# Sample scores as four groups of 24 rows, and both samples of a pair in one pass

## What is computed

```python
gate = einsum('hqd,hnd->hqn', qh, k_mean)              # mean key of each block of 256 keys
_, top = top_k(gate, n_top)                            # the 3 best of 4 past blocks
...
s = einsum('hqd,hqskd->hqsk', qh, kg) * scale
s = s - slopes[:, None, None, None] * (qpos - key_pos) # distance penalty
s = where(valid, s, -inf)
pr = softmax(s.reshape(ATT_HEADS, qc, -1), axis=-1).reshape(s.shape)
return einsum('hqsk,hqskd->hqd', pr, vg)
```

## Time and profile before

| what | value |
|---|---|
| time, median of 3 runs | 1353.81 us (1352.45 to 1355.06) |
| the profiled execution | 1353.38 us |
| its span from first to last instruction | 1351.7 us |
| TensorE busy with matmuls | 1322.9 us, 98% |
| VectorE, ScalarE, GpSimd busy | 57%, 49%, 17% |
| HBM traffic over the span | 173 GB/s |
| mean granted TensorE clock | 0.996 |

### The profile page before, as it was taken

One profiled execution on the slowest core, in us unless ns is written; L12 is line 12 of the kernel. 1 busy time (PEld: TensorE's weight loads), 2 busy tenths in 40 slices (PEclk: granted clock), 3 DMA queues, 4 the chain that ended last, 5 costly groups with the idle time before them and its releaser, 6 DMA issues.

```text
span 1351.7 us, 28355 instructions
## 1 busy us (share of the span) xinstructions
PE 1322.9 (98%) x11129; PEld 1276.1 (94%) x11129; DVE 772.7 (57%) x842; ACT 657.3 (49%) x741; POOL 233.4 (17%) x342
## 2 busy tenths in 40 slices
PE   6999999999999999999999999999999999999998
PEld 5999999999878999999999999999997799999998
DVE  5555555666556655554555555565755565555444
ACT  5555543434444655553355555333443555555434
POOL 4000000356440100000101000013755120000001
PEclk9999999999999999999999999999999999999998
DMA  6655544769787444444446654447797854444443
GB/s 198 206 175 163 167 141 157 191 184 228 184 279 224 143 155 155 142 134 157 158 130 193 186 177 134 156 147 208 182 243 223 255 173 156 140 150 155 141 144 128
DMA packets 213487, 235.27 MB, mean 174 GB/s; under 512 B 15006, under 2 KB 207272, under 8 KB 213396
## 3 DMA queue, kind: packets, MB, share of 16 engines
q1 hardware_dynamic: 205436, 211.19, 51.2%
q0 software_dynamic: 7840, 22.85, 6.0%
q10 hardware_dynamic: 120, 0.03, 0.0%
HBM read 228.83 MB, written 5.32 MB: 173 GB/s over the span
## 4 chain that ended last, share of the span: by engine, by line
PE 92%; issue 5%; DMA 1%; DVE 1%; POOLq 1%; SPq 0%; POOL 0%; ACT 0%; DVEq 0%; ACTq 0%
PE ps L1303 22%; PE ps L1304 22%; PE ps L1305 22%; PE ps L1390 4%; PE ps L1392 4%; PE ps L1391 4%; PE ps L1536 3%; PE ps L1573 2%; PE ps L1710 1%; PE ps L1712 1%; PE ps L1711 1%; PE ps L1431 1%; PE ps L1488 1%; DMA x_tok<-in_x_sample 0%; PE ps L1524 0%
## 5 line engine op out<-in xcount | busy, mean ns | idle before, releaser
L649 ACT ACTIVATE w_hi<-w_raw 128x2048 fp32r<-128x2048 f32 x170 | 325.4, 1914 | 538.6 <-PE ps L1305 421.0
L922 DVE TENSOR_TENSOR w_lo<-w_raw,w_hi 128x2048 fp32r<-128x2048 f32 x162 | 371.9, 2295 | 187.5 <-ACT w_hi L649 185.3
L1303 PE MATMUL ps<-h_hi,w_hi 128*128 128x320 f32 x768 | 239.4, 312 | 4.0 <-DVE x L989 2.3
L1305 PE MATMUL ps<-h_hi,w_lo 128*128 128x320 f32 x768 | 238.3, 310 | 0.0
L1304 PE MATMUL ps<-h_lo,w_hi 128*128 128x320 f32 x768 | 238.2, 310 | 0.0
L1303 PE MATMUL ps<-g_hi,w_hi 128*128 128x320 f32 x704 | 218.0, 310 | 0.0
L1305 PE MATMUL ps<-g_hi,w_lo 128*128 128x320 f32 x704 | 217.5, 309 | 0.0
L1304 PE MATMUL ps<-g_lo,w_hi 128*128 128x320 f32 x704 | 217.5, 309 | 0.0
L1303 PE MATMUL ps<-act_hi,w_hi 128*128 128x320 f32 x704 | 217.4, 309 | 0.0
L1304 PE MATMUL ps<-act_lo,w_hi 128*128 128x320 f32 x704 | 217.4, 309 | 0.0
L1305 PE MATMUL ps<-act_hi,w_lo 128*128 128x320 f32 x704 | 217.4, 309 | 0.0
(11 more groups left out here) (286 smaller groups left out, 1770.7 us busy)
## 6 DMA issues: line engine op xcount, KB each, us to landing
w_raw<-in_ffn_w_in SPq DMA_DIRECT2D x90, 1024.0 KB, 5.1
w_raw<-in_ffn_w_out SPq DMA_DIRECT2D x32, 896.0 KB, 4.6
w_raw<-in_w_in SPq DMA_DIRECT2D x22, 1024.0 KB, 6.0
kbuf<-in_cache_k SPq DMA_DIRECT2D x96, 192.0 KB, 4.9
w_raw<-in_ffn_w_out SPq DMA_DIRECT2D x16, 1024.0 KB, 5.0
kbuf<-in_cache_v SPq DMA_DIRECT2D x64, 192.0 KB, 3.9
w_raw<-in_w_out SPq DMA_DIRECT2D x8, 1024.0 KB, 6.6
kbuf<-in_cache_k POOLq DMA_DIRECT2D x32, 192.0 KB, 3.5
```

The costliest lines, as they stand in the source:

```text
L649: act.activation(w_hi[:, slot, :], w_raw[:, slot, :], ACT.Copy).then_inc(hi_done, 1)
L922: dve.tensor_tensor(w_lo[:, slot, :], w_raw[:, slot, :], w_hi[:, slot, :].bitcast(F32), ALU.subtract).then_inc(split_done, 1)
L1303: pe.matmul(out, w_hi[:, slot, w], hi[:, k, :], start=(k == 0), stop=False)
L1305: ins = pe.matmul(out, w_lo[:, slot, w], hi[:, k, :], start=False, stop=(k == k_all - 1))
```

## The change

- The rows of a pair are laid out as four groups of 32 partitions (sample bb, half of the heads), each with three heads of 8 queries and 8 unused rows: `alibi_s`, `alibi_own`, `rank`, `ss`, `sp` and `o_tok` grow from 96 to 128 partitions. `q_rep`, `q_bd` and `q_sc` get layouts to match; in `qprep`, `q_bd` takes 12 copies of 8 columns in place of 4 of 24.
- `key_scores(p)` and `smp_out(p)` do both samples in one go, on four column groups; the values go by 192 columns (three heads). `own_scores` has 8 matmuls in place of 6.
- `transpose_probs` transposes against all 128 columns of the identity, read with a step, so that the columns of the four groups are interleaved; `smp_out` reads its stationary operand with a step of 4. `transpose_out` becomes six matmuls of 16 columns.
- `sc_done`, `pv_done` and `o_evac` are raised once a pair. `next_k` waits for whole pairs, and SyncE issues `next_k(2, 1)` ahead of `mix_load(9)`.
- Value homes: samples 5 and 6 go to a new home E (`v_e`) and to D, both loaded by GpSimd; the load of sample 5 stands between `spread_v(3)` and `spread_v(4)`. SyncE loads sample 7 alone after pair 1. Both slots of `w_out` are loaded after pair 0.
- TensorE's order: `smp_out(3)` stands behind the first `out_part`, and the `early` parts of slot 1 are placed otherwise.

The constants, tile shapes and index helpers are left out of the diff below.

```diff
...
 
-        q_bd = sb("q_bd", [P, 3, 2, 32])
-        q_rep = sb("q_rep", [P, 4, 3, SMP])
+        q_bd = sb("q_bd", [P, 200])
...
+        v_e = at("v_e", [P, PAGES, HDIM], F32, arena_at, 12)
...
-        v_landed = {n: sem("v_landed_" + n) for n in "CWXABD"}
-        V_HOME = "XWBACDBA"
+        v_landed = {n: sem("v_landed_" + n) for n in "CWXABDE"}
+        V_HOME = "XWBACEDB"
...
-
-            return (6 if p else 4) + bb
+        def out_bank(p):
+
+            return (4, 6, 7, 6)[p]
 
         def page_numbers(engine, first, n):
 
...
 
-                    wait_apart(sp_e, sc_done, L * NB + (1 if p == 1 else p * 2 + (bb - 1)))
+                    wait_apart(sp_e, sc_done, L * (NB // 2) + p)
                     for half in range(2):
                         load_k(p, bb, half)
...
                 mix_load(8)
                 next_k(2, 0)
+                next_k(2, 1)
                 mix_load(9)
-                next_k(2, 1)
                 sp_e.wait_ge(u_out, 2 * L + 2)
                 sp_e.dma_start(O["pool_prompt"][bass.ds(L, 1), 0].rearrange("a t c -> (a t) c"),
...
                             sp_e.dma_start(v_page(u, 4 * half + j, slice(0, HDIM)),
                                            A["cache_v"][L, page[j]].rearrange("t h d -> t (h d)")).then_inc(v_landed[V_HOME[u]], 16)
 
+                wait_apart(sp_e, sc_done, (NB // 2) * L + 4)
                 for u in range(2, 4):
-                    wait_apart(sp_e, sc_done, NB * L + u + 5)
                     load_v(u)
+                wait_apart(sp_e, pv_done, (NB // 2) * L + 1)
                 for slot, cols in enumerate((slice(0, 256), slice(256, 512))):
-                    wait_apart(sp_e, pv_done, NB * L + 1 + slot)
                     square(A["w_out"], L, half0 + C_WO // 2, cols, slot, apart=True)
-                wait_apart(sp_e, pv_done, NB * L + 3)
-                load_v(6)
-                wait_apart(sp_e, pv_done, NB * L + 4)
+                wait_apart(sp_e, pv_done, (NB // 2) * L + 2)
                 load_v(7)
                 sp_e.wait_ge(st_prm, L + 1)
...
                     for bb in range(2):
-                        c = 16 * bb + 8 * half
-                        pool.tensor_copy(q_bd[HD * half:HD * half + HD, :, bb, c:c + 8],
-                                         q_smp[HD * half:HD * half + HD, :, p * 16 + 8 * bb:p * 16 + 8 * bb + 8])
+                        own = q_bd[HD * half:HD * half + HD, 96 * bb + 8 * half:96 * bb + 8 * half + 88]
+                        for f in range(3):
+                            pool.tensor_copy(own[:, 40 * f:40 * f + 8],
+                                             q_smp[HD * half:HD * half + HD, f, p * 16 + 8 * bb:p * 16 + 8 * bb + 8])
                 pool.drain()
-                for half in range(2):
-                    for bb in range(2):
-                        c = 16 * bb + 8 * half
-                        ins = pool.tensor_copy(q_sc[p][:, bb, :, half, :, c:c + 8],
-                                               q_rep[:, 2 * half:2 * half + 2, :, p * 16 + 8 * bb:p * 16 + 8 * bb + 8]
-                                               .rearrange("p j f q -> p f j q"))
+                for bb in range(2):
+                    for gg in range(2):
+                        at_g = 384 * bb + 192 * gg
+                        dst = q_sc[p][:, at_g:at_g + 216].rearrange("p (s x) -> p s x", s=3)[:, :, 0:64]
+                        ins = pool.tensor_copy(dst.rearrange("p s (j c) -> p s j c", j=2)[:, :, :, 0:8],
+                                               q_rep[:, 3 * gg:3 * gg + 3, :, p * 16 + 8 * bb:p * 16 + 8 * bb + 8])
                 ins.then_inc(qp_ok, 1)
 
...
                 spread_v(1)
                 wait_apart(pool, att_low, L + 1)
                 load_v_all(4)
-                for h in range(2, H):
-                    spread_v(h)
+                spread_v(2)
+                spread_v(3)
+                wait_apart(pool, r_done, H * L + H)
+                load_v_all(5)
+                spread_v(4)
+                spread_v(5)
                 wait_apart(pool, vbd_used, H * L + H)
                 wait_apart(pool, pt2_done, NB * L + 4)
-                load_v_all(5)
+                load_v_all(6)
                 add_squares(L * 12 + 8)
                 add_squares(L * 12 + 12)
...
 
-                def out_evac(p, bb):
+                def out_evac(p):
                     act.wait_ge(rs_ok, L * 4 + p + 1)
-                    act.wait_ge(pv_done, L * NB + p * 2 + (bb + 1))
-                    act.activation(o_tok[p % 2][:, bb, :], ps[0:96, out_bank(p, bb), 0:P], ACT.Copy, scale=ss[:, 46 + p:47 + p]).then_inc(o_evac, 1)
+                    act.wait_ge(pv_done, L * 4 + p + 1)
+                    act.activation(o_tok[p % 2][:, :], ps[:, out_bank(p), 0:192], ACT.Copy, scale=ss[:, 46 + p:47 + p]).then_inc(o_evac, 1)
 
                 def y_high(p):
...
                 ret_square(0)
                 act.activation(eps_root[:], eps[:], ACT.Sqrt)
                 ret_square(1)
-                out_evac(0, 0)
-                out_evac(0, 1)
+                out_evac(0)
                 ret_square(2)
                 act.wait_ge(sp_done, L + 1)
                 act.activation(sp_new[:], ps[:, 6, 320:512].rearrange("p (f v) -> p f v", f=3), ACT.Copy).then_inc(st_prm, 1)
                 probs_evac(1)
                 for f in range(3):
                     root_o(f)
-                out_evac(1, 0)
+                out_evac(1)
                 probs_evac(2)
                 y_high(0)
                 exps(3)
-                out_evac(1, 1)
                 mix_hi(12)
-                out_evac(2, 0)
+                out_evac(2)
                 probs_evac(3)
                 for f in range(3):
                     or_high(f)
                 y_high(1)
-                out_evac(2, 1)
                 mix_hi(13)
-                out_evac(3, 0)
                 y_high(2)
-                out_evac(3, 1)
+                out_evac(3)
...
                         pe.matmul(ps[r, 7, :], kr_tok[0:SMP, 2, c], v_bd[h % 2].rearrange("p b v -> p (b v)"),
                                   start=True, stop=True).then_inc(vbd_used, 1)
 
-                def key_scores(p, bb):
-
-                    wait_apart(pe, kt_ok, L * 16 + p * 4 + (2 * bb + 2))
-                    for n in range(4):
-                        a, j = divmod(n, 2)
-                        for f in range(3):
-                            c = (2 * f + a) * HD + 32 * j
+                def key_scores(p):
+
+                    wait_apart(pe, kt_ok, L * 16 + p * 4 + 4)
+                    for n in range(6):
+                        slot, j = divmod(n, 2)
+                        for g in range(4):
+                            c = (3 * (g % 2) + slot) * HD + 32 * j
+                            at_q = 192 * g + 64 * slot + 32 * j
                             for r in range(4):
                                 R = slice(32 * r, 32 * r + 32)
-                                ins = pe.matmul(ps[32 * f:32 * f + 32, 2 + r, 0:256], q_sc[p][R, bb, f, a, j, :],
-                                                kbuf[k_home(p, bb)][R, :, c:c + 32], start=(bb == 0 and n == 0), stop=(bb == 1 and n == 3))
+                                ins = pe.matmul(ps[32 * g:32 * g + 32, 2 + r, 0:256], q_sc[p][R, at_q:at_q + 32],
+                                                kbuf[k_home(p, g // 2)][R, :, c:c + 32], start=(n == 0), stop=(n == 5))
                     ins.then_inc(sc_done, 1)
 
                 def own_scores():
-                    for bb in range(2):
-                        for f in range(3):
-                            ins = pe.matmul(ps[32 * f:32 * f + 32, 5, 256:256 + SMP], q_bd[:, f, bb, :], k_own[:, f, :],
-                                            start=(bb == 0), stop=(bb == 1))
+                    for n in range(2):
+                        for g in range(4):
+                            ins = pe.matmul(ps[32 * g:32 * g + 32, 5, 256:256 + SMP], q_bd[:, 48 * g + 24 * n:48 * g + 24 * n + 32],
+                                            k_own[:, g % 2 + n, :], start=(n == 0), stop=(n == 1))
                     ins.then_inc(own_done, 1)
 
                 def transpose_probs(p):
                     pe.wait_ge(sm_exp, L * 4 + p + 1)
                     if p:
                         pe.wait_ge(pt2_evac, L * 8 + p * 2)
+                    rows = ident[:].rearrange("p (g x) -> p x g", g=4)
+                    to = lambda r, bank, n: ps[r, t_bank(p, bank), 96 * n:96 * n + P].rearrange("p (x g) -> p x g", g=4)
                     for j in range(5):
-                        ins = pe.transpose(ps[:, t_bank(p, 0), 96 * j:96 * j + 96], sp[p][:, P * j:P * j + P], ident[0:96, 0:96])
+                        ins = pe.transpose(to(slice(0, P), 0, j), sp[p][:, P * j:P * j + P], rows)
                     ins.then_inc(pt2_done, 1)
                     for j in range(5, 8):
```

(67 more changed lines are left out.)

51 lines of the change are left out of this document (25 added, 26 removed).

## The result

The changed kernel takes 1384.72 us (median of 4 runs, 1382.66 to 1388.74), the kernel before 1353.13 us in the same runs: ratio 1.0235, interval 1.0209 to 1.0262. I had forecast 1367.5, with 1374 as the upper edge. The direction was right, the size was not: 31.6 us lost where I had 14. The profiled run has a span of 1383.6 us against 1351.7.

The account below looks back on a forecast made before the run. TensorE, 92% of the span, was taken as the bound. 5.15 + 3.65 us up to `smp_out(0)`, 0.1 + 1.05 to `out_part` and 4.0 for the clock made 13.95: 1367.5 us against the median, range 1355 to 1374.

Parts of the forecast that it names:

- chunk 9 was the last to land: Key loads of pair 2: chunk 9, behind sixteen pages, lands last at 337.8 and 996.3, holding TensorE ahead of `att_out(0)`.
- The scores of pair 0: `key_scores`: a cap on records in flight leaves 0.2 us saved a pair, from 4.22 us.
- The chain from `transpose_out(0)` to `out_part`: ScalarE and VectorE work behind `transpose_out(0)` sets `out_part(0)`: from 14.25 to 26.1 us of the stretch, TensorE standing about 5.
- the two signs of being wrong: Wrong if chunk 9 is not last to land, or if the chain behind `y_rest(0)` starts earlier than forecast.
- +0.24 a pair: `transpose_probs`: nine transposes go from 0.80 us at 96 columns to 1.03 to 1.1 at 128.
- my upper bound of 0.5 us a pair for the stepped reads: Stepped reads and weight loads, not shown by the trace at this step: nothing, or 0.5 us a pair.
- The same shift for pair 1 stays hidden: Key loads: the later signal and loads that delay pair 2 cost TensorE nothing at pair 1.
- +5.3 and +3.8: Later start of `att_out(0)` in the two layers, us: TensorE goes on at 340.3 and 998.8, not 334.99 and 995.01.
- Then `smp_out(3)` follows: After `out_part(0)`: `smp_out(3)` at 3.0 for 2.22 us, two `transpose_out` 0.3; stretch +0.1 and +1.05 us.
- my 1.0 us: Slow clock: each of four new idle stretches of 3 to 5 us costs 1.0 us, together 4.0.
- The 0.6 us ahead of `smp_state(2)`: GpSimd, issuing sample 5's value loads between two spreads, is ready at 7.35 where TensorE wants it at 6.8: +0.6 us.
- rival (c): Values of pair 1 are late too, beside GpSimd's pages of sample 5: 1.5 us a layer, 1371; chance 0.1.

Follow-up runs that it names:

- x1: Changed kernel with each pair's `transpose_probs` in another form (identity read in order or stepped, written in order or stepped); only durations count: nine transposes 0.96, 2.13, 2.20, 1.13 us.
- x2: Changed kernel with the identity read in order in `transpose_probs` and the product written with a step of 4 elements: 1379.76 us, ratio 1.0184.
- x8: Changed kernel with `key_scores` cut by sample again, each with its own wait for keys and signal to the key loads: 1374.77 us, ratio 1.0155.
- x5: Changed kernel with VectorE's turn of pair 1's last keys straight behind `turn_k(1, 1, 0)`, ahead of the softmax maxima and evacuation: 1383.74 us, ratio 1.023.
- x4: Changed kernel with `out_part(1, (1,), early)` behind the late part of slot 0 again, and `out_part(1, (0,), ...)` cut around `transpose_out(3)`: 1378.54 us, ratio 1.0178.

## Why the prediction was right in its places and wrong in its size

**Right.** That TensorE would stop being the bound at two places, and which: chunk 9 was the last to land (339.7; I had 337.8) and `out_part` waited for the chain behind `y_rest(0)`. Moving only chunk 9 gave back 9.4 us, moving only the chain 10.2, so both were causes and not only neighbours. The scores of pair 0 were right to 0.1 us, with eight tiles as well. Over all pairs they saved 2.3 us where I had 1.6, but that is in part luck: I had taken the 4.22 us of pair 0 for every pair, and before the change the others took 4.97 to 6.45, with pauses. The chain from `transpose_out(0)` to `out_part` took 11.55 us in both layers; I had 11.85. Neither of the two signs of being wrong that I had named came, so the error lay in terms that I had not named as signs.

**"+0.24 a pair" for `transpose_probs`** was the step that failed most. It cost 1.10, 1.24, 1.33 and 1.33 us for pairs 0 to 3, 10 us of TensorE in two layers against 1.9. I had counted columns, and my upper bound of 0.5 us a pair for the stepped reads came from no row that had one. x1 shows the read alone does it; x2 that 5 us of it reached the end.

**"The same shift for pair 1 stays hidden"** failed. I had followed the loads, which were in time, and not the waiting instruction: `key_scores` now asks for four turned quarters before its first matmul in place of two. 1.55 us in each layer, and with it the signal for the keys of pair 2 and chunk 9 came 5.2 us later where I had 2.3 + 0.6. It is the larger part of why `att_out(0)` starts +7.1 and +6.5 us late, not +5.3 and +3.8. x8 removes the wait; the one other order of VectorE that I tried, x5, did not.

**"Then `smp_out(3)` follows"** ended my sum at `out_part`. I had noted neither that `out_part(1, (1,), early)` was what hid the split of the next chunk (3.5 us in two layers, x4) nor that the matmuls behind the long wait run at half clock for longer than my 1.0 us: `out_part(0)` took 6.34 and 6.71 us against 4.50, 1.84 and 2.21 more. With the 0.76 and 1.01 at `att_out(0)` and its transposes that makes 5.8 us, and `key_scores(2)` behind them took 4.67 and 5.38 us against the 3.94 of pair 0: some 8 us for the clock, not 4.0. I had taken at most 3.4 us at half clock for each place; in three of the four it was 6.8.

**Smaller ones.** `smp_out` takes 3.24 us, not 3.0. `qprep` held TensorE 0.7 us, not 0.9. The 0.6 us ahead of `smp_state(2)` did not show, presumably because the slow transposes came first (in x2, where they are fast, 0.23 us stands there). Of rival (c) a part came true: one wait of 1.1 us for the values of pair 1, in layer 1 only. That the wait for `sp_c` would grow to 0.76 us I had not looked for. And 1353.81 + 13.95 is 1367.8, not 1367.5.

The sum by stages: up to `smp_out(0)` 10.8 us forecast with its clock, 16.3 measured; from there to the end of `out_part` 3.2 forecast, 14.8 measured. In the second, `transpose_out(0)` came at 16.2 and 17.4 us where I had 14.25, by the slow transposes and, in layer 1, the wait for values; the rest is the clock, the `w_lo` wait and the slower calls at its end. Open are the pauses inside `key_scores`, which no run explains.

## What to carry to other kernels

A loop that merges two halves merges their waits: ask what each first instruction needs now, and what engine was working under the first half. When a change takes work out of the bound engine, the chain that comes next starts at the same event as before, so list for each stage its second-longest chain with its start, and look past the last call that the diff moved for what that call had been hiding. And price an access pattern by a row with that pattern or call its cost unknown; here two lines, which put the step on the written side, gave back 5 us.

## What the runs showed of the hardware

A transpose on TensorE whose moving operand was read with a step of 4 or of 32 float32 elements took 0.24 us for 128 columns where one in order took 0.12; a step of 4 on the PSUM side cost nothing (x1). On 32x32 tiles, records of 256 columns came at 27, 22 and 20.5 ns with 8, 12 and 16 tiles in use, in calls without a pause. Around the four waits of 4.1 to 4.6 us the granted clock was 0.50 (1.2 GHz) for 3.4 us once and 6.8 us three times, and in those three it fell before the wait had ended. After the 1.55 us ahead of `key_scores(1)` it stayed at 1.00, while before the change it was 0.50 after 1.17 us; the length of the wait alone does not tell.
